# A two-block hybrid kernel on one core: the feed-forward computed token by token with its norm by halves, and the delta rule's output steps spread between attention work

## The chip, the cores and the metric

The kernel runs on one core of a Trainium2 chip. The metric is the time of one execution in microseconds on the device. Three executions of the kernel before gave 1759.13, 1759.20 and 1759.99 us, median 1759.2 us.

## The reference, cut to what matters

A first block of two layers (gated delta rule, latent attention and a gated linear recurrence side by side, then an output projection), then a second block of two layers, each with two feed-forwards around a mixer. There are 256 tokens of 1024 features, all in float32.

```python
# first block, in each layer: the delta rule in chunks
v_new = u_n - w_n @ state                       # per head
o = (q_n * exp(g_n)) @ state + a_n @ v_new
state = state * exp(g_last) + (k_n * exp(g_last - g_n)).T @ v_new
o_a = rmsnorm(o, gdn_out_norm) * silu(gz)
...
o_b = causal_block_attention(qf, kf, vm) * silu(mz)
x = x + concatenate([o_a, o_b, o_c]) @ w_out

# second block, in each layer l
x = x + 0.5 * swiglu(rms_norm(x, ffn1_norm[l]), gate, up, down)    # f10, f11
mem_n = rms_norm(mem, mem_norm[l])
...
x = x + mixed @ w_out[l]
x = x + 0.5 * swiglu(rms_norm(x, ffn2_norm[l]), gate, up, down)    # f20, f21
```

A swiglu is `(silu(h @ gate) * (h @ up)) @ down` with a hidden width of 2816, which the kernel takes as 11 blocks (`PAIRS`) of 256 columns. The first block's result also goes through `final_norm` before the second block reads it.

## The kernel before

The whole program is one list of steps, written out by hand in `schedule()`. Every engine walks the same list in the same order and does its own part of each step, so the list is at the same time the instruction order of TensorE, VectorE, ScalarE and GpSimd. Semaphores tie the engines together; an engine that waits holds up everything behind it in its own order.

Every float32 product with a weight is done as three products of reduced-width parts. A block of weights (1 MB) lands in `ring`; ScalarE rounds it into `weights_high` (two instructions, one for each half of the block), VectorE subtracts that from the original into `weights_rest` (again two), and TensorE multiplies high by high, high by rest and rest by high. `weights_high` has three places (`HIGHS`), the ring four, and five from the second block on. How far ScalarE and VectorE are ahead with this splitting is said at each step by `split_until(n)`: "everything up to block n, if not yet done".

Activations lie transposed, as 8 slices of 128 features by 256 tokens (`xT_high`, `xT_rest`). A norm step takes the mean square of both halves of the tokens (128 each), scales both, transposes both on TensorE (16 transposes), and then ScalarE and VectorE write the slices 256 tokens wide.

The feed-forward of before works feature by feature: block `g` (gate) and block `u` (up) give 256 hidden features by 256 tokens, each from 48 products that move 256 tokens past a piece of weights; ScalarE does the silu of `g`, VectorE multiplies by `u`, rounds (`CAST`) and subtracts, and the block `d` (down) is added into four PSUM banks by 24 products of 512 columns. On TensorE the down products of block j-1 stand behind gate and up of block j:

```python
for j in range(begin, pairs + 1 if end == pairs else end):
    ... gate and up of block j
    if j: ... pe.wait_ge(*at((id, "h", i))); accumulate(... i = j - 1 ...)
```

ScalarE's and VectorE's part of block j begins, for every j, with `split_until(split_no[(st, "g", j)] + 3)`. For j = 0 this is gate 0, up 0 and gate 1; for later j it is gate j, up j and down j-1. In `f10` and `f11` the norm of the memory tokens stands between the blocks: `norm_front` (squares, scales) ahead of block 5, and `norm_part` behind blocks 5 to 8.

The delta rule's output (`gdn_o`, once for each half n of the tokens) was one step each: on TensorE u, S and o for n = 0, or u, w, wS and o for n = 1, then the sum of squares of o. Between these products stand copies of PSUM results by ScalarE and one subtraction by VectorE. Attention of the first block has the steps `att` (scores; on VectorE mask and maximum), `sm` (exponential, division) and `pv` (transposes, values), and `mz` is a projection of 48 products.

In the profile's rows all ordinary products have line 784, transposes of a norm line 842, those of `pv` line 1147, the splitting on VectorE line 1889, and everything of ScalarE line 1377.

Of the kernel before, what the change touches and what calls it, by code (L numbers as in the profile page):

```python
# [16 lines left out]
F32 = mybir.dt.float32  # L17
F32R = mybir.dt.float32r
U32 = mybir.dt.uint32
ALU = mybir.AluOpType  # L20
# [3 lines left out]
P = 128  # L24
# [120 lines left out]
PAIRS = DFF // 256  # L145

# [6 lines left out]
def schedule():  # L153

    out = []
    for l in range(2):
        out.append(("norm", f"n{l}", "x", f"norm_gain{l}"))
        out.append(("ab", l))
        def proj(name, j=0):
# [10 lines left out]
                  32: (rots[0:3], rots[3:5]), 64: ([proj("mz", 0)], [])}  # L170
        out += [("tri", l, 0, 1), ("trid", l, 0, 1), proj("gz", 1), ("tri", l, 1, 1), ("trid", l, 1, 1)]
        for s in LEVELS[1:]:
            for n in range(2):
                out += [("tri", l, n, s)] + beside[s][n] + [("trid", l, n, s)]
        m = f"m{l}"
# [65 lines left out]
def weight_blocks(w):  # L241
# [12 lines left out]
    for st in schedule():  # L254
# [21 lines left out]
        elif kind == "ffn" and st[2] == 0:  # L276
# [71 lines left out]
def two_blocks(nc, w, out, old):  # L348
# [5 lines left out]
    half_at = block_no[(("ffn", "f10"), "g", 0)]  # L354
# [40 lines left out]
    with ctx:  # L395
# [251 lines left out]
        SLICES = (2, 3, 0, 1, 4, 5, 6, 7)  # L647

# [54 lines left out]
        def _(sp_eng):  # L703
# [6 lines left out]
            mem_at = block_no[(("ffn", "f10"), "g", 4)]  # L710
            for i, (key, pieces, _) in enumerate(blocks):
# [13 lines left out]
                if key == (("ffn", "f11"), "g", 4):  # L725
# [17 lines left out]
        def _(eng):  # L743
# [56 lines left out]
            def first_block(id, key, gkey, wv):  # L800

                banks = [group((*gkey, f)) for f in range(2)]
                wh_, wl_ = wv
                for n, k in enumerate(SLICES):
                    pe.wait_ge(*at(("xh", id, k)))
                    if k >= 4:
                        second_half(key)
                    for f in range(2):
                        for i, a in enumerate((wh_, wl_)):
                            mm(banks[f][:, 0:S], a[:, k, f * P:f * P + P], xh[:, k, :], n == 0 and i == 0, False)  # L810
                for n, k in enumerate(SLICES):
                    need_slice(n)
                    for f in range(2):
                        ins = mm(banks[f][:, 0:S], wh_[:, k, f * P:f * P + P], xl[:, k, :], False, n == KD - 1)
                ins.then_inc(*pe.mark(gkey, used=key))

# [13 lines left out]

            def st_norm(st):
# [3 lines left out]

                gs = [k // 2 for k in slices_of(st)[::2]]
                b = {g: group(("nt", id, g), among=range(4, 8) if id in ("f10", "f20", "f21") else None) for g in sorted(gs)}
# [156 lines left out]
            def st_gdn_o(st):  # L994
# [6 lines left out]
                ins.then_inc(*pe.mark(("u", l, n)))  # L1001
                if n == 0:
# [6 lines left out]
                else:  # L1009
                    pe.wait_ge(*at(("TTg", l)))  # L1010
                    b = group(("w", l))
                    for h in range(4):
                        ins = mm(b[:, h * P:h * P + P], ktm[:, 1, h, :], ET[:, 1, h, :])
                    ins.then_inc(*pe.mark(("w", l)))
                    pe.wait_ge(*at(("wT", l)))
                    pe.wait_ge(*at(("St", l)))
                    b = group(("wS", l))
# [1542 lines left out]
```

## Time and profile before

| | |
|---|---|
| median of three executions | 1759.2 us |
| the profiled execution, its own time | 1756.48 us |
| its span, first to last instruction | 1754.7 us |
| mean granted clock of TensorE | 0.974 |
| TensorE busy | 1661.3 us (95%) |
| VectorE busy | 1048.1 us (60%) |
| ScalarE busy | 872.9 us (50%) |

The span is nearly the time itself, and TensorE is busy in 95% of it. So the profile is read for the places at which TensorE has no work, for how fast its products follow each other where it has, and for its clock. In a timeline row the first number is the start and the second the duration in us; a duration includes the tail of the last product, so the rate of a stream is read from starts. The bracket gives the idle time just before, and what ended it.

### The profile page before, as it was taken

The page shows a single profiled execution, that of the slowest core. Times are in us where ns is not written, and L with a number is a line of the kernel's source. Part 1 is how long each engine was busy: PE and PEld are TensorE (multiplying, and loading weights), DVE is VectorE, ACT ScalarE, POOL GpSimd, SP SyncE. Part 2 cuts the span into 40 slices and gives each one's busy share as a digit, 9 for nine tenths or more (in the row PEclk, how much of TensorE's full clock was granted, in tenths as well). Part 3 has the DMA queues.
Part 4 walks back from the last instruction along what each step waited for, and adds up shares of the span by engine and source line. Part 5 has one row for each costly group of instructions (what it writes and reads, how often), then busy time and mean ns, then how long its engine had stood idle before and what let it go on. Part 6 is the DMA issues. An engine that isn't in the chain of part 4 may idle for free.

```text
span 1754.7 us, 27203 instructions
## 1 busy us (share of the span) xinstructions
PE 1661.3 (95%) x11578; PEld 1531.1 (87%) x11578; DVE 1048.1 (60%) x1506; ACT 872.9 (50%) x1297; POOL 97.7 (6%) x72
## 2 busy tenths in 40 slices
PE   7999899999989899999888999999999998789999
PEld 7989777989977799999887899989999997679998
DVE  6875564896646555555786645455646465555554
ACT  4975363686445435435445533344454357443332
POOL 0112000012200000000240000000000000000000
PEclk9999999999999899999999999998999999899999
DMA  7624224552313465555321555544665553035552
GB/s 224 191 66 135 71 73 145 157 158 89 97 49 117 163 213 191 171 190 169 121 83 62 168 186 179 188 140 135 196 204 175 185 169 120 24 113 179 190 192 97
DMA packets 204297, 253.24 MB, mean 144 GB/s; under 512 B 17808, under 2 KB 183952, under 8 KB 204048
## 3 DMA queue, kind: packets, MB, share of 16 engines
q1 hardware_dynamic: 204176, 251.49, 44.9%
q8 instruction: 92, 1.51, 0.4%
q14 instruction: 29, 0.24, 0.0%
HBM read 250.43 MB, written 1.05 MB: 143 GB/s over the span
## 4 chain that ended last, share of the span: by engine, by line
PE 78%; DVE 8%; ACT 6%; issue 5%; DMA 1%; POOL 1%; SPq 0%; DVEq 0%; ACTq 0%; POOLq 0%
PE bank L784 77%; ACT arena L1377 4%; DVE weights_rest L1889 2%; ACT weights_high L1377 1%; PE bank L842 1%; DVE arena L2036 1%; DMA ring<-in_w_in 1%; ACT L1377 1%; ACT L1372 1%; DVE small L2206 0%; DVE x L2252 0%; DVE weights_rest_more L1889 0%; DVE arena L2224 0%; POOL arena L2520 0%; DMA vec<-in_vec 0%
## 5 line engine op out<-in xcount | busy, mean ns | idle before, releaser
L784 PE MATMUL bank<-xT_high,weights_high 128*128 128x256 f32 (+1 forms) x2352 | 676.1, 288 | 8.9 <-DVE weights_rest L1889 4.1
L784 PE MATMUL bank<-xT_rest,weights_high 128*128 128x256 f32 (+1 forms) x2352 | 658.3, 284 | 0.0
L784 PE MATMUL bank<-xT_high,weights_rest 128*128 128x256 f32 (+1 forms) x2048 | 581.4, 285 | 0.0
L1889 DVE TENSOR_TENSOR weights_rest<-ring,weights_high 128x1024 fp32r<-128x1024 f32 (+3 forms) x414 | 486.6, 1225 | 98.8 <-ACT weights_high L1377 95.1
L1377 ACT ACTIVATE weights_high<-ring 128x1024 fp32r<-128x1024 f32 (+3 forms) x414 | 400.6, 1019 | 253.9 <-PE bank L784 235.6
L784 PEld LDWEIGHTS bank<-xT_high,weights_high 128*128 128x128 f32 (+1 forms) x2352 | 454.2, 193 | 19.4 <-issue 8.9
L784 PEld LDWEIGHTS bank<-xT_rest,weights_high 128*128 128x128 f32 (+1 forms) x2352 | 448.1, 192 | 3.5 <-issue 2.0
L784 PEld LDWEIGHTS bank<-xT_high,weights_rest 128*128 128x128 f32 (+1 forms) x2048 | 395.7, 193 | 0.6
L1377 ACT ACTIVATE arena<-bank 128x512 f32<-128x512 f32 (+4 forms) x253 | 134.5, 547 | 390.3 <-PE bank L784 327.4
L784 PE MATMUL bank<-arena 128*128 128x128 f32 (+2 forms) x1416 | 209.4, 307 | 37.3 <-ACT arena L1377 22.9
L784 PEld LDWEIGHTS bank<-arena 128*128 128x128 f32 (+1 forms) x1416 | 180.2, 203 | 63.6 <-ACT arena L1377 22.6
L2289 DVE TENSOR_TENSOR arena<-bank,arena 128x512 f32<-128x512 f32 x44 | 30.4, 692 | 321.3 <-PE bank L784 321.3
L784 PE MATMUL bank<-weights_high,arena_parts 128*128 128x512 f32 (+1 forms) x416 | 112.3, 379 | 0.9 <-DVE arena L2235 0.9
L784 PE MATMUL bank<-weights_high,hidden_high 128*128 128x512 f32 x352 | 96.3, 391 | 0.0
L784 PE MATMUL bank<-weights_high,hidden_rest 128*128 128x512 f32 x352 | 95.5, 389 | 0.0
L1377 ACT ACTIVATE weights_high<-ring_more 128x1024 fp32r<-128x1024 f32 x68 | 68.3, 1056 | 53.2 <-PE bank L784 53.1
L784 PEld LDWEIGHTS bank<-weights_high,arena_parts 128*128 128x128 f32 x416 | 76.4, 191 | 15.2 <-DVE arena L2235 1.0
L1889 DVE TENSOR_TENSOR weights_rest_more<-ring_more,weights_high 128x1024 fp32r<-128x1024 f32 x68 | 82.5, 1253 | 8.8 <-ACT weights_high L1377 7.9
L784 PE MATMUL bank<-xT_high,weights_rest_more 128*128 128x256 f32 x304 | 86.0, 283 | 0.0
L784 PEld LDWEIGHTS bank<-weights_high,hidden_rest 128*128 128x128 f32 x352 | 66.1, 188 | 14.2
L784 PE MATMUL bank<-weights_rest,hidden_high 128*128 128x512 f32 x272 | 73.4, 389 | 0.0
L784 PEld LDWEIGHTS bank<-weights_high,hidden_high 128*128 128x128 f32 x352 | 63.5, 189 | 11.1
(180 smaller groups left out, 1698.1 us busy)
## 6 DMA issues: line engine op xcount, KB each, us to landing
ring<-in_w_in SPq DMA_DIRECT2D x36, 1024.0 KB, 5.2
ring<-in_ffn_w_gate SPq DMA_DIRECT2D x36, 1024.0 KB, 5.4
ring<-in_ffn_w_up SPq DMA_DIRECT2D x35, 1024.0 KB, 5.4
ring<-in_ffn_w_down SPq DMA_DIRECT2D x34, 1024.0 KB, 4.9
ring<-in_w_out SPq DMA_DIRECT2D x22, 1024.0 KB, 4.9
ring<-in_w_in_a SPq DMA_DIRECT2D x11, 1024.0 KB, 5.2
ring_more<-in_ffn_w_down SPq DMA_DIRECT2D x10, 1024.0 KB, 5.1
ring_more<-in_ffn_w_up SPq DMA_DIRECT2D x9, 1024.0 KB, 5.3
```

Of the source, the lines that this page charges most:

```text
L784: return eng.matmul(o, a, b, start=first, stop=last)
L842: ins = eng.transpose(b[g][:, kk * S + t * P:kk * S + t * P + P], xs_of(st)[:, t, (2 * g + kk) * P:(2 * g + kk + 1) * P], ident)
L1372: eng.preload_act_table_set(need)
L1377: return eng.activation(dst, src, func, **kw_)
L1889: TTs(rest_slot(b)[:, part], raw_slot(b)[:, part], high_slot(key)[:, part].bitcast(F32), ALU.subtract).then_inc(*dv.mark(("rest", key, z)))
L2036: STT(out=cq[:, i, :], in0=cin[:, i, j:j + S], scalar=taps[:, j:j + 1], in1=cq[:, i, :], op0=ALU.mult, op1=ALU.add).then_inc(*dv.mark(*((( ...
L2289: TTs(h, ps(g, 2, S), h, ALU.mult).then_inc(*dv.mark((id, "h32", j), frees=g))
```

## The change

1. `schedule()`: `gdn_o` is cut into `gdn_u` (u, and w for n = 1), `gdn_w` (wS), `gdn_o` (S and o) and `gdn_n` (the norm of o), and `att` into `sc` (scores on TensorE) and `att` (the rest) for the first two head pairs. These steps are put between others.
2. Feed-forward: gate and up of a block come as two weight blocks (`g, j, 0` and `g, j, 1`), each with 4 of the 8 slices, 256 gate and 256 up columns side by side. The product is turned around: 128 tokens are the stationary side, and 512 weight columns move past them. The hidden values come out token by token and are transposed (4 transposes a block). ScalarE rounds them from PSUM, VectorE subtracts.
3. The norms ahead of `f10`, `f20` and `f21` are done by halves of the tokens: add, scale, transpose and slices of the first half, then its products of block 0, then the same for the second half. The norm ahead of `f11` stays as it was.
4. For block 0, ScalarE and VectorE now split 2 weight blocks ahead instead of 3.

```diff
-        out += [("gdn_o", l, 0), ("att", m, 0), ("sm", m, 0), proj("mz", 1), ("gdn_o", l, 1)]
+        out += [("gdn_u", l, 0), ("att", m, 0), ("sm", m, 0), proj("mz", 1), ("gdn_o", l, 0), ("gdn_u", l, 1)]
+        out += [("sc", m, 1), ("gdn_n", l, 0), ("gdn_w", l)]
...
+            if hp == 1:
+                out[-3:] = [("gdn_o", l, 1), ("sm", m, 1), proj("mz", 2), ("gdn_n", l, 1), ("parts", f"h{l}", *ready[1])]
...
-                cols((st, "g", j), w[f"{n}_w_gate_2"][l], 256 * j, 256 * j + 256)
-                cols((st, "u", j), w[f"{n}_w_up_2"][l], 256 * j, 256 * j + 256)
+                for z in range(2):
+                    pieces = [(w[f"{n}_w_{name}_2"][l].rearrange("(k p) n -> p k n", p=P)[:, 4 * z:4 * z + 4, 256 * j:256 * j + 256], c, c + 256)
+                              for name, c in (("gate", 0), ("up", 256))]
+                    out.append(((st, "g", j, z), pieces, (4, 512)))
...
+            def gate_up(st, j, z, t, b, order):
...
+                for n, k in order:
+                    if j == 0 and id in BY_TOKENS.values():
+                        pe.wait_ge(*at(("xl", id, t, k)))
+                    else:
+                        need_slice(n)
+                    if k % 4 >= 2:
+                        second_half(key)
+                    for i, (a, v) in enumerate(products(wv, [xh, xl])):
+                        ins = mm(b[:, 0:512], v[:, k, t * P:t * P + P], a[:, k % 4, :], n == 0 and i == 0, n == KD - 1 and i == 2)
...
+                for j in range(begin, end):
+                    b = [group((id, "gu", j, t)) for t in range(NT)]
+                    if j == 0 and id in BY_TOKENS.values():
...
+                        transposes(id, 1)
...
+                    else:
+                        for z in range(2):
+                            for t in range(NT):
+                                gate_up(st, j, z, t, b[t], order[4 * z:4 * z + 4])
+                            if j and z == 0:
+                                hidden_transposes(st, j - 1)
+                    if j == 1:
+                        open_acc(st)
+                    if j and j < pairs - 1:
+                        down(st, j - 1, (0, 1), (0, 1), used=True)
...
                 for j in range(begin, end):
-                    g = (id, "g", j)
-                    split_until(split_no[(st, "g", j)] + 3)
...
+                    split_until(split_no[(st, "g", j, 0)] + (3 if j else 2))
+                    if j:
+                        hidden_high(st, j - 1)
+                    for t in range(NT):
+                        g = (id, "gu", j, t)
+                        copy(sg[:, j % 2, t, :], g, ps(g, 2, S)[:, 0, :], (id, "s", j, t), func=ACT.Silu)
...
+            def add_and_norm(st, id):
...
+                add(0)
+                scale(0)
+                if id == "f20":
+                    split_until(n, more=1)
+                    slices(0, SLICES)
+                    add(1)
+                else:
+                    slices(0, SLICES[:4])
+                    add(1)
+                    split_until(n, more=1)
+                    slices(0, SLICES[4:])
+                split_until(n, more=2)
+                scale(1)
+                slices(1, SLICES)
```

**Order 1.** ScalarE (ACT) in `f21`, from the end of its norm to the silu of block 1. `weights_high` is the splitting; `arena2<-bank` is a silu (in before of gate alone, in after of each half of the tokens). Before:

```order
L1377 ACTIVATE weights_high<-ring 128x1024 [waits landed0,pe_outp]
L1377 ACTIVATE weights_high<-ring 128x1024
L1377 ACT_TABLE_LOAD
L1377 ACTIVATE arena2<-bank1 128x256 [waits pe_ffn]
L1377 ACTIVATE arena2<-bank2 128x256
L1377 ACTIVATE weights_high<-ring 128x1024 [waits landed1]
L1377 ACTIVATE weights_high<-ring 128x1024
L1377 ACTIVATE weights_high<-ring 128x1024 [waits landed2,pe_ffn]
L1377 ACTIVATE weights_high<-ring 128x1024
L1377 ACTIVATE arena2<-bank0 128x512 [waits pe_ffn]
```

The changed kernel, at the same place:

```order
L1430 ACT_TABLE_LOAD
L1430 ACTIVATE arena2<-bank1 128x256
L1430 ACTIVATE arena2<-bank2 128x256 [waits pe_ffn]
L1430 ACTIVATE weights_high<-ring 128x1024 [waits landed0,pe_outp]
L1430 ACTIVATE weights_high<-ring 128x1024
L1430 ACTIVATE weights_high<-ring 128x1024 [waits landed1]
L1430 ACTIVATE weights_high<-ring 128x1024
L1430 ACTIVATE weights_high<-ring 128x1024 [waits landed2]
L1430 ACTIVATE weights_high<-ring 128x1024
L1430 ACTIVATE hidden_high<-bank1 128x512 [waits pe_ffn]
```

The split of the weights that block 1 begins with (gate 1 before, `g, 1, 0` now) stood ahead of the first silu and stands behind both now. VectorE's order has moved in the same way.

**Order 2.** ScalarE in `f10` of the changed kernel, around `norm_front`, ahead of block 5. The first two rows are the silus of block 4, the last the rounded hidden values of block 4.

```order
L1430 ACTIVATE arena2<-bank0 128x256 [waits pe_ffn]
L1430 ACTIVATE arena2<-bank1 128x256 [waits pe_ffn]
L1425 ACT_TABLE_LOAD
L1430 ACTIVATE arena2,small<-arena2 128x1024 [waits mem_in]
L1430 ACTIVATE small<-small 128x1 [waits act_norm_front] x2
L1430 ACTIVATE arena2,small<-arena2 128x1024 [waits act_norm_front]
L1430 ACTIVATE small<-small 128x1 [waits act_norm_front] x2
L1430 ACTIVATE weights_high<-ring_more 128x1024 [waits landed4,act_norm_front]
L1430 ACTIVATE weights_high<-ring_more 128x1024
```

Before, the same work stood behind a silu that waited for gate alone; now it stands behind one that waits for gate and up of the whole block.

**Order 3.** TensorE (PE) at the delta rule's output, layer 0, 128x128 float32 products (`bank<-arena`), from u and w of the second half on. Before:

```order
L784 MATMUL bank6<-arena 128x128 [waits dve_trid]
L784 MATMUL bank6<-arena 128x128 x3
L784 MATMUL bank7<-arena 128x128 [waits dve_trid]
L784 MATMUL bank7<-arena 128x128 x3
L784 MATMUL bank0<-arena 128x128 [waits act_gdn_o]
L784 MATMUL bank0<-arena 128x128 x3
L784 MATMUL bank1<-arena 128x128 [waits dve_gdn_a,dve_gdn_o]
L784 MATMUL bank1<-arena 128x128 x7
L784 MATMUL bank2<-arena,const 128x512 [waits act_gdn_o]
```

The changed kernel, from S and o of the first half (banks 3 and 4) to the second transposes of `pv`:

```order
L791 MATMUL bank4<-arena 128x128 x4
L791 MATMUL bank5<-arena 128x128 [waits dve_trid]
L791 MATMUL bank5<-arena 128x128 x3
L791 MATMUL bank6<-arena 128x128 [waits dve_att,dve_trid]
L791 MATMUL bank6<-arena 128x128 x3
L791 MATMUL bank7<-arena 128x128 [waits dve_att]
...
L791 MATMUL bank1<-arena,const 128x512 [waits act_gdn_o]
L791 MATMUL bank2<-arena 128x128 [waits act_proj,act_gdn_o]
L791 MATMUL bank2<-arena 128x128 x3
L1166 MATMUL bank3<-const,arena 128x128 [waits dve_sm]
L1166 MATMUL bank3<-const,arena 128x128
L1166 MATMUL bank4<-const,arena 128x128 [waits dve_gdn_o,dve_sm]
```

The scores (banks 7 and 0) now stand between w and wS (bank 2), the values of pair 0 between wS and o; and the last row takes bank 4, in which o of the first half lies until VectorE has read it.

## Rows read from the trace of the kernel before

**Rows 1.** The page: its head and the engines' busy time

```profile
span 1754.7 us, 27203 instructions
...
PE 1661.3 (95%) x11578; PEld 1531.1 (87%) x11578; DVE 1048.1 (60%) x1506; ACT 872.9 (50%) x1297; POOL 97.7 (6%) x72
```

**Rows 2.** Windows, in f21: PE, PEld, DVE, ACT, POOL busy, clock, DMA share, GB/s

```profile
1650.00:1675.00 25.00, 25.00 (x176) 23.51 (x176) 11.59 (x14) 10.39 (x11) 0.00 (x0) 1.00 0.57 186
```

**Rows 3.** TensorE's timeline in f21: down, gate and up, the next down

```profile
1654.88 1.09 PE L784 MATMUL bank<-weights_high,hidden_high 128*128 128x512 f32 x4
...
1660.34 0.28 PE L784 MATMUL bank<-xT_high,weights_high 128*128 128x256 f32 x1
...
1671.86 1.09 PE L784 MATMUL bank<-weights_high,hidden_high 128*128 128x512 f32 x4
```

**Rows 4.** TensorE's timeline: products after an idle stretch

```profile
978.73 1.94 PE L842 MATMUL bank<-const,arena 128*128 128x128 f32 x16 [3.27 <-DVE arena L1956]
...
1170.95 2.70 PE L842 MATMUL bank<-const,arena 128*128 128x128 f32 x16 [3.27 <-DVE arena L1956]
...
1560.53 3.14 PE L842 MATMUL bank<-const,arena 128*128 128x128 f32 x16 [3.27 <-DVE arena L1956]
```

**Rows 5.** Timelines of ScalarE and VectorE: a split of one block; a silu

```profile
1549.30 1.99 ACT L1377 ACTIVATE weights_high<-ring 128x1024 fp32r<-128x1024 f32 x2
...
1550.37 2.36 DVE L1889 TENSOR_TENSOR weights_rest<-ring,weights_high 128x1024 fp32r<-128x1024 f32 x2 [0.52 <-ACT weights_high L1377]
...
1569.88 0.66 ACT L1377 ACTIVATE arena<-bank 128x256 f32<-128x256 f32 x2 [1.47 <-PE bank L784]
```

**Rows 6.** ScalarE's timeline in f10 around the front of the memory norm

```profile
674.64 0.60 ACT L1377 ACTIVATE arena<-bank 128x512 f32<-128x512 f32 x1 [3.80 <-PE bank L784]
675.26 1.28 ACT L1372 ACT_TABLE_LOAD   x1
...
680.05 2.01 ACT L1377 ACTIVATE weights_high<-ring_more 128x1024 fp32r<-128x1024 f32 x2
```

**Rows 7.** Timelines at the starts of f10, f20 and f21, TensorE and VectorE

```profile
591.19 1.29 DVE L2252 SCALAR_TENSOR_TENSOR x<-bank,x 128x512 f32<-128x512 f32 x2 [4.79 <-PE bank L784]
...
598.18 1.63 PE L842 MATMUL bank<-const,arena 128*128 128x128 f32 x8 [4.28 <-DVE arena L2309]
...
604.00 0.55 PE L784 MATMUL bank<-xT_high,weights_high 128*128 128x256 f32 x1 [1.16 <-DVE xT_high L1977]
...
629.21 1.09 PE L784 MATMUL bank<-weights_high,hidden_high 128*128 128x512 f32 x4
...
973.43 1.28 DVE L2252 SCALAR_TENSOR_TENSOR x<-bank,x 128x512 f32<-128x512 f32 x2
...
1003.79 1.09 PE L784 MATMUL bank<-weights_high,hidden_high 128*128 128x512 f32 x4
...
1554.57 1.29 DVE L2252 SCALAR_TENSOR_TENSOR x<-bank,x 128x512 f32<-128x512 f32 x2 [1.83 <-PE bank L784]
...
1586.96 1.09 PE L784 MATMUL bank<-weights_high,hidden_high 128*128 128x512 f32 x4
```

**Rows 8.** Timelines at the delta rule's output, layer 0, TensorE and VectorE

```profile
192.49 2.05 PE L784 MATMUL bank<-arena 128*128 128x128 f32 x16 [0.75 <-ACT arena L1377]
195.23 2.05 PE L784 MATMUL bank<-arena 128*128 128x128 f32 x16 [0.69 <-ACT arena L1377]
197.97 1.12 PE L784 MATMUL bank<-arena,const 128*128 128x512 f32 x2 [0.69 <-ACT arena L1377]
...
201.87 0.69 DVE L2162 TENSOR_TENSOR arena<-bank,arena 128x512 f32<-128x512 f32 x1 [6.17 <-ACT arena L1377]
...
213.22 2.07 PE L784 MATMUL bank<-arena 128*128 128x128 f32 x8 [2.42 <-ACT arena L1377]
216.14 3.71 PE L784 MATMUL bank<-arena 128*128 128x128 f32 x16 [0.85 <-DVE arena L2155]
220.53 1.13 PE L784 MATMUL bank<-arena,const 128*128 128x512 f32 x2 [0.69 <-ACT arena L1377]
```

More of the change, by code:

```diff
@@ L647, in two_blocks @@
         SLICES = (2, 3, 0, 1, 4, 5, 6, 7)
+        BY_TOKENS = {"h1": "f10", "s0": "f20", "s1": "f21"}
         def slices_of(st):
@@ L834, in st_norm @@
                     eng.wait_ge(sems("ident_in"), 16)
+                if id in BY_TOKENS.values():
+                    transposes(id, 0)
+                    return
                 gs = [k // 2 for k in slices_of(st)[::2]]
-                b = {g: group(("nt", id, g), among=range(4, 8) if id in ("f10", "f20", "f21") else None) for g in sorted(gs)}
+                b = {g: group(("nt", id, g)) for g in sorted(gs)}
                 for t in range(NT):
@@ L1415, in st_final @@
                 for t in range(NT):
[L1416 to L1417 removed]
+                    one = slice(t, t + 1)
+                    ac.wait_ge(*at(("x_ready", id, t)))
+                    A(final_sq if id == "f10" else xs2[:, t, :], x[:, t, :], ACT.Square, accum_out=ss[:, one]).then_inc(*ac.mark(("ss", id, t)))
                     ac.wait_ge(*ac.last())
[L1419 removed]
@@ L1877, in split_until @@
             def split_until(n, ahead=0, more=0):
-                n = 2 * min(reach((pieces[0] + 1) // 2, n, ahead), len(split)) + more
+                n = 2 * min(reach((pieces[0] + 1) // 2, n, ahead) if ahead else n, len(split)) + more
                 while pieces[0] < n:
@@ new lines, in add_acc, with slices, add @@
+            def add_acc(st, scale):
+                added = [add_half(st, t, scale) for t in range(NT)]
+                for nx in sched[place[st] + 1:]:
+                    if nx[0] == "norm" and nx[2] == "x":
+                        for t in range(NT):
+                            new.at[("x_ready", nx[1], t)] = added[t]
+                        break
+            def add_and_norm(st, id):
+                gain = next(nx[3] for nx in sched if nx[0] == "norm" and nx[1] == id)
+                n = (pieces[0] + 1) // 2 + 1
+                split_until(n)
+                def slices(t, ks):
+                    for k in ks:
+                        v = ps(("nt", id, t, k // 2), 2, P)
+                        src, g = v[:, k % 2, :], V(gain)[:, k:k + 1]
+                        to = slice(t * P, t * P + P)
+                        if k == 2:
+                            dv.wait_ge(*at(("nt", id, t, 1)))
+                            for q in (2, 3):
+                                TS(xh[:, q, to], v[:, q % 2, :], V(gain)[:, q:q + 1], None, ALU.mult).then_inc(*dv.mark())
+                            dv.wait_ge(*dv.last())
+                        if k not in (2, 3):
+                            dv.wait_ge(*at(("xh", id, t, k)))
+                            dv.wait_ge(*at(("xh", id, t, k ^ 1)))
+                        STT(out=xl[:, k, to], in0=src, scalar=g, in1=xh[:, k, to].bitcast(F32), op0=ALU.mult,
+                            op1=ALU.subtract).then_inc(*dv.mark(("xl", id, t, k), frees=("nt", id, t, k // 2)))
+                def add(t):
+                    new.at[("x_ready", id, t)] = add_half(st, t, 1.0)
+                    if id == "f10":
```

337 lines of the change are left out of this document (181 added, 156 removed).

## The prediction

> **What bounds the kernel.** I read the page first: TensorE is busy for 95% of the span and no other engine for more than 60% [rows 1]. Then the windows: inside a feed-forward TensorE is busy for 25.00 of 25 us at full clock, while VectorE and ScalarE have less than half of the time filled and the transfers 0.57 of theirs [rows 2]. So a steady block costs what TensorE's instructions cost, and everything else is a matter of places where TensorE has nothing to do. Those I took from its timeline: before the norms of f10, f20 and f21 [rows 7], and in the delta rule's output [rows 8]. After an idle stretch comes a second price: the same 16 transposes behind the same 3.27 us of idling took 1.94, 2.70 and 3.14 us [rows 4], since the clock had sometimes fallen to its lower level.
>
> **Steady blocks.** From 1654.88 to 1660.34 TensorE does the 24 products of down, 0.2275 us each; from there to 1671.86 the 96 products of gate and up with 256 columns, 0.120 us each, 11.52 us together [rows 3]. The new gate and up are 48 products of 512 columns, of the shape of down: 48 x 0.2275 = 10.92 us. That saves 0.60 us a block. It adds 4 transposes of 128x128: 16 took 1.94 us warm, of which about 0.28 is the tail of the last [rows 3, 4], so 0.11 each and 0.44 a block. 44 blocks in four feed-forwards; three block 0s are counted with the starts below: 41 x 0.60 = 24.6 saved, 44 x 0.44 = 19.4 paid, **-5.2 us**. The Trainium skill has this otherwise (TensorE: Matmul & The Clock Gate, section Back-to-back issue gap): 262 cycles for 256 columns and 518 for 512, or 0.109 and 0.216 us at 2.4 GHz. By that gate and up would go from 10.5 to 10.4 us, 0.1 saved instead of 0.6, and 41 blocks would be some 20 us dearer than in my sum. The row has 0.120 for 256 columns, so I keep the row.
>
> In the steady state nothing else reaches TensorE, as I lay it out. The weights of the next block are split behind the silu that ends a block, 0.33 + 3.43 us (below), under 5.46 us of down. Hidden values have 5.4 us of second-half gate and up over them. At the end of a feed-forward the rounding and subtraction, some 1.3 us, lie beside 6 products of down (1.37 us); uncovered they would cost 5 us in all. The transfers are 88 more issues of half the size, with the landing one ring place ahead and the queue idle most of the time: no cost, and 0.4 us each if they ever stood in line.
>
> **Block 1 of each feed-forward.** Here I see a new wait. Order 1: the split of the weights of block 1 stands behind both silus of block 0, on ScalarE and on VectorE, and TensorE's first product takes slice 2, for which it asks for both halves of the split. Down begins only behind block 1, so between block 0 and block 1 TensorE has nothing at all. The chain: silu of the second half 0.33 us (half of 0.66), then ScalarE's start to VectorE's end of one block 1549.30 to 1552.73, 3.43 us [rows 5]; with signals 3.8 us. Before, gate 1 was split ahead. Four times 15.2 us. After 3.8 us of idling the clock probably falls. What that costs: in the transposes alone 0, 0.76 and 1.20 us in the three cases of [rows 4], and in the delta rule 2.7 us (below). I take 1.7, with 0 and 2.7 as ends: 6.8 us. Together **+22.0 us**. The queue behind this wait on TensorE is all of the feed-forward; nothing hides it.
>
> **Block 5 of f10 and f11.** Order 2: the front of the memory norm stands on ScalarE between the silu of block 4 and the split for block 5. From the end of the silu at 675.24 to the start of the split at 680.05 it takes 4.81 us [rows 6]. It used to follow the silu of gate, with up (5.76 us) and down (5.46) still before TensorE; now it follows the end of the whole block. 0.33 + 4.81 + 3.43 = 8.6 us against 5.46 us of down: 3.1 us of wait, and 1.7 for the clock: twice, **+9.6 us** (6.2 without the clock, 11.6 with 2.7).
>
> **The starts by halves.** f10 idles 4.28 + 1.06 + 1.16 us before its first product, f20 and f21 3.27 us before their transposes [rows 4, 7]. Block 0 was finished 11.52 us before the first down: 617.69, 992.27 and 1575.44 [rows 7]. In the new order the first half goes from its add (591.19, 973.43, 1554.57) through square, scale, 8 transposes and slices, and TensorE starts its 24 products about 6 to 7 us after the add in f10, where the gain of the final norm is multiplied in, and 5 to 6 in the others; but VectorE does add, split and slices of both halves one after the other, so the second half's transposes come only 15 us (f10) and 12 us behind the add, and 24 x 0.2275 = 5.5 us of products behind those. That ends block 0 at about 613.4, 992.3 and 1573.5: **-6.2 us** in all (f10 -4.3, f20 0, f21 -1.9). The ends: 0, and all of the idling above, 13 us. For f20 the add starts late, behind a split, and in the new order it is followed by one more split piece and all eight slices before the second half's add; so I expect nothing there. f11 keeps its norm but loses the pass over the high parts that began before the rests were ready: **+0.5**.
>
> **The delta rule's output.** Before, TensorE waits 0.75 + 0.69 + 0.69 + 2.42 + 0.85 + 0.69 = 6.09 us in a layer, and runs slowly for a while: the 8 records of wS take 2.07 us where 16 took 2.05, the 16 of o 3.71 [rows 8], so 1.0 + 1.7 = 2.7 us more. 8.8 us a layer; the second layer shows the same rows. Order 3: the scores (16 records) and the projections now cover the first four waits and the last. But the second transposes of pv take bank 4, where o of the first half lies until VectorE has read it. From the end of the sum of squares at 199.09 to VectorE's start at 201.87 are 2.78 us, and 0.69 for the reading [rows 8]; wS and two transposes cover 1.3 of these 3.5 us. Then o of the second half waits for wS to be subtracted, on VectorE behind the whole norm of the first half. I put 3.0 us of waits and 1.2 of slow clock (between 0 and 2.7): 4.6 us gained a layer, **-9.2 us** (ends -5 and -17.6).
>
> **Sum.** -5.2 + 22.0 + 9.6 - 6.2 + 0.5 - 9.2 = +11.5 us. The profiled execution took 1756.48 us, 1.8 more than its span, so it would take 1768.0; the median of the runs is 2.7 us above it, and 1759.2 + 11.5 = 1770.7 us.
>
> **Rivals.**
> - Clock unhurt: the six new waits are there but the clock stays up. As after 978.73, where 16 transposes took 1.94 us [rows 4]; against it are the other two cases and longer waits now. 11.5 - 10.2 = +1.3: 1760.5 us.
> - Faster: block 1 isn't starved. If the split of its weights were finished while TensorE is still in the second half of block 0, 22.0 us fall away: 1748.7 us. It decides where wait and clock together cost less than 2.6 us in a feed-forward instead of 5.5. For it: only three short instructions are in the chain. Against: Order 1 puts them behind a silu that needs the last product of block 0.
> - Every block starved: 3.8 us of chain under 5.46 us of down leave 1.7 us. If the new order (silu in two parts, rounding on ScalarE) makes the chain 0.5 us too long, 36 blocks cost 18 us: 1789 us. Against it: ScalarE has 10.39 us of work in 25 [rows 2].
> - Turned products no cheaper: 256 columns pace at their 512-column rate, so gate and up saves 0.1 us a block; 20 us dearer, 1791 us. That is the rule above; the row speaks against it.
>
> **How the numbers follow.** About 0.2%, 3.5 us, can be told from no change. Forecast (waits of 3 to 4 us with clock, partial gains): 0.56, its own range 1763 to 1779. Clock unhurt 0.16, faster rival 0.12, every block starved 0.12, no cheaper products 0.04. The range leaves out the faster rival's centre and the last two: 1751 to 1787. Faster: the rival's 0.12, some of the case with the clock up and of larger gains in the starts and the delta rule, 0.20. Same 0.14, slower 0.66.
>
> **What would show it.** A block period (down to down) of 16.8 us instead of 16.98. An idle stretch of about 3.8 us before the first product of block 1 in each of four feed-forwards, released by VectorE's split, and of about 3.1 us ahead of block 5 in f10 and f11. In the delta rule one wait of about 2.2 us inside pv's transposes, released by VectorE, and no 2.42 us wait. First downs of f10 and f21 would be 2 to 5 us earlier relative to the output projection, were there no wait before block 1. I am wrong if TensorE runs through from block 0 to block 1, or if the block period isn't below 16.98.

## The result and the profile after

Five executions of the changed kernel took 1764.13 to 1767.94 us, median 1765.56; five of the kernel before, in the same comparison, 1751.16 to 1759.99, median 1759.13. The ratio is 1.0048, with a 95% interval of 1.0025 to 1.0071: slower, by 6.4 us of median against the 11.5 that I had forecast. The execution that was profiled took 1767.94 us, 11.5 more than the profiled one of before. Two later comparisons of the same two kernels gave 1.0104 and 1.0095 (below), so the cost is somewhere from 6 to 17 us, and the first comparison shows the low end of it. The forecast lies between them.

The page of the changed kernel, its head and busy times, to be read beside [rows 1]:

```profile
span 1766.0 us, 23513 instructions
...
PE 1659.5 (94%) x9642; PEld 1437.4 (81%) x9642; DVE 1044.2 (59%) x1536; ACT 904.0 (51%) x1399; POOL 97.7 (6%) x72
```

TensorE has 1936 instructions fewer: 48 products in place of 96 in each of 44 blocks, less four transposes added to each. Its busy time falls by only 1.8 us, since the products that are left have twice the columns, and 0.2275 us each instead of 0.120 [rows 3]. The mean granted clock hardly moved, 0.972 against 0.974. A stretch inside f21, of the same length as [rows 2], as windows (columns as there):

```profile
1625.00:1650.00 25.00, 25.00 (x116) 20.69 (x115) 9.65 (x11) 8.51 (x13) 0.00 (x0) 1.00 0.55 184
```

The steady state is as before: TensorE is full, at full clock. The list of what TensorE waited for (engine and line, the total in us, how often, the longest) shows what is new:

```profile
PE bank L791 <- DVE weights_rest L1968: 14.0, 5, 3.9
PE bank L791 <- DVE weights_rest_more L1968: 11.5, 4, 3.9
...
PE bank L1166 <- DVE arena L2244: 5.0, 2, 2.5
```

Waits for split weights took 4.1 us in all before and take 25.5 now. TensorE's timeline in f10, between block 0 and block 1:

```profile
598.84 0.39 PE L791 MATMUL bank<-weights_rest,xT_high 128*128 128x512 f32 x1
603.13 0.63 PE L791 MATMUL bank<-weights_high,xT_high 128*128 128x512 f32 x1 [3.91 <-DVE weights_rest L1968]
603.56 0.63 PE L791 MATMUL bank<-weights_high,xT_rest 128*128 128x512 f32 x1
```

3.9 us without work, and then a product every 0.43 us instead of 0.2275. ScalarE and VectorE at the same place:

```profile
599.26 0.38 ACT L1430 ACTIVATE arena<-bank 128x256 f32<-128x256 f32 x1 [2.27 <-PE bank L791]
599.54 3.88 ACT L1430 ACTIVATE weights_high<-ring 128x1024 fp32r<-128x1024 f32 x4
...
600.63 4.63 DVE L1968 TENSOR_TENSOR weights_rest<-ring,weights_high 128x1024 fp32r<-128x1024 f32 x4 [0.52 <-ACT weights_high L1430]
```

The silu of block 0's second half starts when TensorE has stopped, and the split of block 1's weights comes behind it: the chain of the forecast, piece by piece. The windows of the wait, of what follows, and of the next 10 us:

```profile
599.23:603.13 3.90, 0.00 (x0) 0.03 (x1) 2.93 (x4) 3.87 (x5) 0.00 (x0) 1.00 1.08 361
603.13:606.55 3.42, 3.42 (x9) 2.68 (x9) 3.42 (x4) 2.19 (x3) 0.00 (x0) 0.52 0.31 102
606.55:616.20 9.65, 9.65 (x45) 7.98 (x44) 2.09 (x3) 0.98 (x2) 0.00 (x0) 0.99 0.34 110
```

The third number from the right is the granted clock: 0.52 of full speed for 3.4 us behind the wait, then full again. The same timeline ahead of block 5, ScalarE first, then TensorE:

```profile
666.80 0.38 ACT L1430 ACTIVATE arena<-bank 128x256 f32<-128x256 f32 x1 [2.34 <-PE bank L791]
667.21 1.28 ACT L1425 ACT_TABLE_LOAD   x1
...
671.99 2.00 ACT L1430 ACTIVATE weights_high<-ring_more 128x1024 fp32r<-128x1024 f32 x2
...
671.14 1.07 PE L791 MATMUL bank<-weights_rest,hidden_high 128*128 128x512 f32 x4
675.59 0.77 PE L791 MATMUL bank<-weights_high,xT_high 128*128 128x512 f32 x1 [3.38 <-DVE weights_rest_more L1968]
```

Where the 11.3 us between the two spans lie, stage by stage, from starts in the two timelines, with an output projection taken at the end of its last product. "First" and "last down" are the first products of down behind block 1 and block 10:

| stage | before | after | difference |
|---|---|---|---|
| start to last output projection of the first block | 593.90 | 579.81 | -14.1 |
| from there to f10's first down | 35.31 | 36.40 | +1.1 |
| f10, first to last down | 154.55 | 159.71 | +5.2 |
| mixer, layer 0 | 191.25 | 193.65 | +2.4 |
| from there to f20's first down | 28.78 | 34.67 | +5.9 |
| f20, first to last down | 152.82 | 151.22 | -1.6 |
| f20's last down to f11's first | 92.29 | 98.46 | +6.2 |
| f11, first to last down | 154.56 | 158.39 | +3.8 |
| mixer, layer 1 | 153.35 | 152.58 | -0.8 |
| from there to f21's first down | 30.15 | 34.15 | +4.0 |
| f21, first to last down | 152.82 | 151.22 | -1.6 |
| f21's last down to the end | 14.92 | 15.74 | +0.8 |

### The profile page after: what moved, and what is told of

Read it like the earlier page. It is cut to its first block, busy times and chain, and to the rows that moved or that the text cites. A ratio compares the mean times of both kernels' runs of the same rounds, so it can differ in the third digit from the quotient of the medians.

```text
span 1766.0 us, 23513 instructions
## 1 busy us (share of the span) xinstructions
PE 1659.5 (94%) x9642; PEld 1437.4 (81%) x9642; DVE 1044.2 (59%) x1536; ACT 904.0 (51%) x1399; POOL 97.7 (6%) x72
## 4 chain that ended last, share of the span: by engine, by line
PE 56%; DVE 6%; ACT 4%; issue 1%; POOL 1%; DVEq 0%; ACTq 0%; POOLq 0%
PE bank L791 54%; ACT arena L1430 2%; DVE weights_rest L1968 2%; PE bank L1220 1%; DVE weights_rest_more L1968 1%; ACT weights_high L1430 1%; PE bank L847 1%; ACT L1425 0%; DVE small L2288 0%; DVE x L2333 0%; POOL arena L2649 0%; DVE xT_rest L2365 0%; DVE arena L2306 0%; DVE arena L2528 0%; POOL arena L2648 0%
## 5 line engine op out<-in xcount | busy, mean ns | idle before, releaser
L791 PE MATMUL bank<-weights_high,xT_high 128*128 128x512 f32 (+2 forms) x880 | 340.7, 393 | 34.8 <-DVE weights_rest_more L1968 11.5
L791 PE MATMUL bank<-weights_high,xT_rest 128*128 128x512 f32 (+2 forms) x816 | 311.0, 381 | 0.0
L791 PE MATMUL bank<-xT_high,weights_high 128*128 128x256 f32 (+1 forms) x944 | 276.8, 293 | 6.0 <-DVE xT_rest L2062 3.1
L791 PE MATMUL bank<-xT_rest,weights_high 128*128 128x256 f32 (+1 forms) x944 | 269.6, 286 | 0.0
L791 PE MATMUL bank<-weights_rest,xT_high 128*128 128x512 f32 (+2 forms) x696 | 262.3, 383 | 0.0
L791 PE MATMUL bank<-xT_high,weights_rest 128*128 128x256 f32 (+1 forms) x912 | 260.4, 285 | 0.0
L791 PE MATMUL bank<-arena 128*128 128x128 f32 (+3 forms) x1416 | 204.2, 304 | 29.4 <-ACT arena L1430 17.1
L791 PEld LDWEIGHTS bank<-xT_high,weights_high 128*128 128x128 f32 (+1 forms) x944 | 182.4, 193 | 13.4 <-issue 6.2
L791 PEld LDWEIGHTS bank<-xT_rest,weights_high 128*128 128x128 f32 (+1 forms) x944 | 182.3, 193 | 2.4 <-issue 2.0
L791 PEld LDWEIGHTS bank<-xT_high,weights_rest 128*128 128x128 f32 (+1 forms) x912 | 175.8, 193 | 0.6
L791 PEld LDWEIGHTS bank<-weights_rest,xT_high 128*128 128x128 f32 x696 | 133.7, 192 | 25.6
L1430 ACT ACTIVATE hidden_high<-bank 128x512 fp32r<-128x512 f32 x44 | 26.3, 599 | 166.8 <-PE bank L1220 166.8
```

The source lines that it names most:

```text
L791: return eng.matmul(o, a, b, start=first, stop=last)
L1430: return eng.activation(dst, src, func, **kw_)
```

## The experiments

The ratios are to the kernel before, measured beside it on the same chip. There were three chips. The two repairs, both together and the filler ran on the first. The changed kernel again, the two runs on the delta rule's part and the one on the bank of o ran on the second. The changed kernel a third time, both repairs again and the last two experiments ran on the third.

### One more block split ahead in block 0

```diff
-                    split_until(split_no[(st, "g", j, 0)] + (3 if j else 2))
+                    split_until(split_no[(st, "g", j, 0)] + 3)
```

> The kernel after, with one number changed: in block 0 of each feed-forward ScalarE and VectorE split three weight blocks ahead instead of two, so that the first weight block of block 1 is ready before block 0 ends. My theory (block 1 is starved by this split, and the clock falls behind the wait): the idle 3.90 us and the slow 1.6 us behind it go in all four feed-forwards, so 22 us less than after, about 1744 us and a ratio to before near 0.991. Rival 1 (the third split goes on ScalarE between the norm's slices and the silu and delays the start of block 0 or the silu by as much as it saves): within 5 us of after, 1761 to 1766. Rival 2 (the wait goes, the clock does not come back): 15.6 us less, about 1750.

Median 1745.2 us, ratio 0.9967 (0.9954 to 0.9981). Against the changed kernel's 1.0104 and 1.0095 that is 1.3% or 23 us less: my theory. (The expected ratio of 0.991 was missed only because the kernel before took 1752.0 us here, not 1759.) TensorE's timeline at block 1 of f10 has:

```profile
599.58 0.39 PE L791 MATMUL bank<-weights_rest,xT_high 128*128 128x512 f32 x1
601.02 0.47 PE L791 MATMUL bank<-weights_high,xT_high 128*128 128x512 f32 x1 [1.06 <-DVE weights_rest L1968]
```

1.06 us are left in f10, where ScalarE also does the final norm, and none in the other three; the products behind it come at full rate. In the trace the four stages that end at a first down are 4.2, 3.8, 6.6 and 5.8 us shorter; of f11's 6.6, 0.8 lie ahead of its norm, so the start itself gained 5.8 as well. f20 gets only 3.8, since in this execution the clock fell earlier, in block 0. Two windows of f20:

```profile
967.53:971.94 4.41, 4.41 (x10) 3.45 (x11) 3.99 (x10) 1.63 (x5) 0.00 (x0) 0.50 0.07 26
971.94:993.60 21.66, 21.23 (x99) 17.41 (x98) 12.48 (x21) 10.57 (x18) 0.00 (x0) 1.00 0.44 146
```

### One block split ahead of the memory norm's front

```diff
+                if st[2] == "mem":
+                    split_until(splits[0] + 1)
```

(on ScalarE; VectorE has the same with its own counter)

> The kernel after, with one weight block more split ahead of the front of the memory norm in f10 and f11 on ScalarE and VectorE (behind the silu of block 4, before the squares). My theory (block 5 is starved because its split stands behind 4.8 us of norm): the two idles of 3.38 us and the slow stretches behind them (2.9 and 1.7 us) go, 11 us less than after, about 1754 us. Rival (the norm's front is then late and delays a later block or the memory transposes by the same): no more than 3 us less than after.

Median 1758.72, ratio 1.0043 (1.0032 to 1.0055), 0.57% or 10 us less than the changed kernel in the two later comparisons. Both waits are gone, and first to last down takes 153.18 and 153.16 us in f10 and f11 instead of 159.71 and 158.39: 11.8 us. At block 5 TensorE's timeline now runs through:

```profile
669.72 1.07 PE L791 MATMUL bank<-weights_rest,hidden_high 128*128 128x512 f32 x4
670.62 0.39 PE L791 MATMUL bank<-weights_high,xT_high 128*128 128x512 f32 x1
```

### Both

> The kernel after with both edits: three weight blocks ahead in block 0 of each feed-forward, and one ahead of the front of the memory norm. My theory adds the two: 33 us less than after, about 1733 us, a ratio to before near 0.985. Rival (the two share something, such as weight blocks that land too late when both are split early): less than 28 us.

Median 1737.03, ratio 0.9917 (0.9905 to 0.9929). Once more, with the changed kernel on the same chip:

> Both repairs once more (three weight blocks ahead in block 0, one ahead of the memory norm's front), beside the next kernel on one chip. Ratio 0.992, as the first time; between 0.989 and 0.994 if only the clock's differences from one execution to the next are added.

Median 1737.93, ratio 0.9910 (0.9896 to 0.9923), against 1770.99 of the changed kernel: 33.1 us less. The two repairs add, 23 and 10 us; the difference is the expected 33, and the expected 1733 us was counted from the first comparison's lower median of the changed kernel, 1765.56.

### The wait filled with products

```diff
+                    if j == 1:
+                        for _ in range(16):
+                            mm(b[0][:, 0:512], xh[:, 0, 0:P], xh[:, 0:2, :].rearrange("p a b -> p (a b)"))
```

> The kernel after with work added and no wait taken away: ahead of block 1 of each feed-forward TensorE does 16 more products of 512 columns (about 3.6 us) whose result is overwritten by the block's own first product, so they lie inside the wait of 3.90 us. If the slow 1.6 us behind the wait come from the idling, the clock stays up and the kernel gains up to 6 us over after, about 1760 us. If the clock does not hang on the idling, or the slow records are something else, the time is that of after within 1 us.

TensorE's timeline, and the windows of the filler and of what follows:

```profile
597.31 3.79 PE L791 MATMUL bank<-xT_high 128*128 128x512 f32 x16
601.38 0.47 PE L791 MATMUL bank<-weights_high,xT_high 128*128 128x512 f32 x1 [0.28 <-DVE weights_rest L1971]
601.69 0.40 PE L791 MATMUL bank<-weights_high,xT_rest 128*128 128x512 f32 x1
```

```profile
597.31:601.10 3.79, 3.79 (x17) 2.82 (x15) 2.65 (x3) 3.59 (x5) 0.00 (x0) 1.00 1.07 356
601.38:605.00 3.62, 3.62 (x16) 3.02 (x17) 3.62 (x4) 2.20 (x3) 0.00 (x0) 1.00 0.31 102
```

The weights come as late as before, but the clock stays at 1.00 in all four places, and the three starts that begin behind an output projection are 1.6 us shorter each. Median 1765.02, ratio 1.0072 (1.0059 to 1.0085), 0.28% or 5 us under the changed kernel in its two later comparisons. So the slow stretch belongs to the idling: filling the wait with useless work wins back the price of the slow stretch, though not the wait.

### The changed kernel again

> The kernel after once more, unchanged, so that the kernels of this call stand against it on one chip. Its ratio to before was 1.0048 (1.0025 to 1.0071); the sum of the two profiled executions gives 1.0064. The mechanical account (waits and clock read from the traces) gives +11 us, a ratio of 1.0063; if the earlier interval's centre is right, 1.0048.

> The kernel after a third time, unchanged. Its two comparisons so far gave 1.0048 and 1.0104, with intervals that do not meet, while its own median moved little (1765.6 and 1769.4) and that of before moved more (1759.1, 1752.0, 1752.9). Theory: the mean granted clock differs from one execution to the next (0.970 to 0.980 for the same kernel before), 0.001 of it is about 1.7 us, and the result of one comparison carries some 5 us of that. Then this gives a ratio between 1.005 and 1.011. If a property of the first session alone was the cause, 1.010 again.

Medians 1769.37 and 1770.99, ratios 1.0104 (1.0083 to 1.0125) and 1.0095 (1.0079 to 1.0110). The interval of the first comparison doesn't meet either. The kernel before had medians of 1752.0, 1752.85 and 1754.2 us on the three chips of the experiments (38 executions) and 1759.13 in the first comparison, where four of its five lay at 1757.85 to 1759.99 and one at 1751.16. Among the 38 the time goes with the mean granted clock: 1760.74 us at 0.971 and 1760.23 at 0.970, 1749.13 to 1753.84 in the executions at 0.979; a straight line through all 38 gives 1.0 us for 0.001 of clock, not the 1.7 expected above. The profiled execution of before had 0.974, and the clocks of the others in the first comparison aren't on record. So it is likely, not shown, that part of the difference between the comparisons is how often the clock fell in the kernel before; the changed kernel's own median also rose, by 3.8 and 5.4 us. The third ratio, 1.0095, fits both of the expectations above and doesn't decide between them. What set the first comparison apart stays open.

### The delta rule's part alone, and all but it

In the kernel before:

```diff
-        out += [("gdn_o", l, 0), ("att", m, 0), ("sm", m, 0), proj("mz", 1), ("gdn_o", l, 1)]
+        out += [("gdn_u", l, 0), ("att", m, 0), ("sm", m, 0), proj("mz", 1), ("gdn_o", l, 0), ("gdn_u", l, 1)]
+        out += [("sc", m, 1), ("gdn_n", l, 0), ("gdn_w", l)]
```

with all the steps and functions that this needs, and in the changed kernel:

```diff
-        out += [("gdn_u", l, 0), ("att", m, 0), ("sm", m, 0), proj("mz", 1), ("gdn_o", l, 0), ("gdn_u", l, 1)]
-        out += [("sc", m, 1), ("gdn_n", l, 0), ("gdn_w", l)]
+        out += [("gdn_u", l, 0), ("gdn_o", l, 0), ("gdn_n", l, 0), ("sc", m, 0), ("att", m, 0), ("sm", m, 0), proj("mz", 1)]
+        out += [("gdn_u", l, 1), ("gdn_w", l), ("gdn_o", l, 1), ("gdn_n", l, 1), ("sc", m, 1)]
```

> The kernel before with the first part of the change alone: the delta rule's output and the scores cut into steps and spread; feed-forward and norms as before. If the gain of the delta rule that the traces show (7.4 and 6.7 us in the two layers) is its own, this is 14 us faster than before, a ratio of 0.992. If my prediction's size (4.6 a layer) is right, 9 us, 0.995. If part of the gain came from the feed-forward's change or from the chip's drift, less than 9.

> The kernel after without the first part of the change: the steps of the delta rule's output stand as in the kernel before, feed-forward and norms as after. If the parts add, this is 14 us slower than after, 25 us slower than before, a ratio of 1.014; by my prediction's sizes 20.7 us slower than before, 1.012.

The spread alone: median 1743.45, ratio 0.9945 (0.9928 to 0.9963), 9.4 us of median less than before. Without it: 1779.17, ratio 1.0153 (1.0127 to 1.0178), 9.8 us more than the changed kernel on the same chip. That is my forecast's 9.2, not the 14 that the traces suggested. The traces of the two kernels without the spread come from executions 3.6 and 4.3 us above their medians (1756.48 against 1752.85, 1783.45 against 1779.17), which would be most of the gap. For the second the place shows: in its trace the clock is low from 213.0 to 230.1 us, and the stretch between the first layer's early and late output projections takes 83.6 us, against 79.3 in before and 73.8 in the changed kernel. For the first it stays an argument. The rest of the change, then, costs 25.9 us (1743.45 to 1769.37), or 26.3 (1752.85 to 1779.17), where I had 20.7. TensorE's timeline of the changed kernel at the first pv, and VectorE's read that lets it go on:

```profile
210.93 0.38 PE L1166 MATMUL bank<-const,arena 128*128 128x128 f32 x2
213.81 0.77 PE L1166 MATMUL bank<-const,arena 128*128 128x128 f32 x4 [2.50 <-DVE arena L2244]
...
231.67 1.57 PE L791 MATMUL bank<-arena 128*128 128x128 f32 x12 [0.97 <-ACT arena L1430]
...
212.97 0.69 DVE L2244 TENSOR_TENSOR arena<-bank,arena 128x512 f32<-128x512 f32 x1 [8.38 <-ACT arena L1430]
```

The third row is a wait that before didn't have, 0.97 us ahead of the values of the second pv, released by ScalarE. o of the second half doesn't wait: it follows the values of the first pv without a gap. Together this is 3.5 us of wait a layer where there were 6.09 [rows 8].

### The transposes off the bank of o

```diff
-                    b = group(("pt", name, hp, t))
+                    b = group(("pt", name, hp, t), among=[i for i in range(8) if i != new.bank[("o", int(name[1]), 0)]] if (name[0], hp) == ("m", 0) else None)
```

> Both repairs of the feed-forward (three weight blocks ahead in block 0, one ahead of the memory norm's front) and, in the delta rule, the transposes of the first pv kept out of the PSUM bank that holds o of the first half. The wait of 2.50 us before pv's second transposes is released by VectorE's reading of that bank: if the bank is its cause it goes in both layers, 5 us less than with the repairs alone, a ratio of about 0.989 instead of 0.992. Rival: another bank or VectorE's next read holds it as long, and nothing changes, 0.992.

Median 1734.68, ratio 0.9906 (0.9886 to 0.9926), the same as without it. TensorE's timeline:

```profile
210.78 0.82 PE L1166 MATMUL bank<-const,arena 128*128 128x128 f32 x6
213.57 1.60 PE L791 MATMUL bank<-arena 128*128 128x128 f32 x12 [1.97 <-DVE arena L2248]
216.09 1.16 PE L791 MATMUL bank<-arena 128*128 128x128 f32 x8 [0.91 <-DVE arena L2238]
```

All six transposes run on, and the values behind them wait for the same read of VectorE (1.97 us), then o for VectorE's subtraction (0.91). One bank later the same thing is late; the wait is moved, not removed. What this trace does differently is the clock: it stays at 1.00 behind both waits in both layers, and the layers are 1.1 and 1.0 us shorter for it. The timed runs don't tell whether that is the edit's doing or this execution's.

### A projection ahead of pv

```diff
             if hp == 1:
-                out[-3:] = [("gdn_o", l, 1), ("sm", m, 1), proj("mz", 2), ("gdn_n", l, 1), ("parts", f"h{l}", *ready[1])]
+                out[-4:] = [proj("mz", 2), ("pv", m, 0), ("gdn_o", l, 1), ("sm", m, 1)]
+            if hp == 2:
+                out[-4:-4] = [("gdn_n", l, 1), ("parts", f"h{l}", *ready[1])]
```

> Both repairs, and in the first block two steps moved: the third mz projection (48 products, some 11 us) goes ahead of the first pv, and the norm of o of the second half goes behind the scores of the third head pair. If the waits of 2.50 and 0.97 us in each layer come from VectorE standing behind the norm of o's first half, they are covered: 7 us less than with the repairs alone, 0.988. If the steps moved leave another wait of the same length (the pv products behind ScalarE's exponential, or the sum of squares behind its square), 0.992 again.

A miss: median 1745.03, ratio 0.9945 (0.9931 to 0.9960), 7.1 us more than the repairs alone on the same chip. TensorE, then ScalarE:

```profile
229.03 0.82 PE L1168 MATMUL bank<-const,arena 128*128 128x128 f32 x6
234.51 1.86 PE L793 MATMUL bank<-arena 128*128 128x128 f32 x7 [4.66 <-ACT arena L1432]
...
233.13 1.06 ACT L1432 ACTIVATE arena_parts<-arena 128x1024 fp32r<-128x1024 f32 x1 [1.46 <-DVE arena L2253]
234.09 0.85 ACT L1432 ACTIVATE arena<-bank 128x256 f32<-128x256 f32 x2
```

The wait at the first pv went (0.31 us is left), but the rounding of the delta rule's output (`parts`), which must follow its norm, now stands ahead of ScalarE's copies for the second pv, and itself waits for VectorE: 4.66 us where 0.97 had been. So a layer waits 4.97 us instead of 3.47, 3.0 us more in the two. In the trace the two layers' stretches are 1.5 and 2.5 us longer than with the repairs alone; the 1.0 beyond the waits is the clock's, which was low for 6.8 us in the second layer's stretch instead of 3.4. The trace's other 3.8 us lie in its first 130 us, where no step was moved and where traces of the same code differ as much (128.3 to 132.5 us). What makes up the last 3 of the 7 us in the timed runs stays open.

### Halves for f10 alone

```diff
-        BY_TOKENS = {"h1": "f10", "s0": "f20", "s1": "f21"}
+        BY_TOKENS = {"h1": "f10"}
...
-                    split_until(splits[0] + (1 if id == "s0" else 2))
+                    split_until(splits[0] + 2)
```

> The kernel after with the norm by halves kept for f10 alone; the norms ahead of f20 and f21 are done as in the kernel before, 16 transposes and slices 256 tokens wide (and ScalarE splits two weight blocks behind the last output projection of s0, as in before). The terms of my sum for these two starts are 0 and -1.9 us, so this is 1.9 us slower than after, and the stretch from the output projection to the first down of f20 stays within 0.5 us. If the halves are worth the idle of 3.27 us that they replace, 4 to 5 us slower. If by halves is dearer there (more transposes in pieces, more waits), 1 to 3 us faster.

Median 1773.53, ratio 1.0114 (1.0100 to 1.0128) beside the changed kernel's 1.0095 (1.0079 to 1.0110): the intervals touch. The traces say it more finely: to f20's first down 34.82 us instead of 34.67, to f21's 35.89 instead of 34.15, where block 0 ends 18.7 us behind the projection instead of 17.0. The halves are worth nothing in f20 and 1.7 us in f21.

## Why the prediction was right

- **Block 1 of each feed-forward (+22.0).** Right in mechanism and size. The wait was 3.90 us in all four (I had 3.8), released by VectorE's split, and the slow stretches behind cost 1.6 us each (I had 1.7): 22.0 us. Counted from starts it is 5.8 us a place, 23.2 in all, because the tail of the last product ahead of the wait and the first products behind it cost another 0.3, which I had left out. Shown by the first experiment, and the clock's share of it by the filler. The rivals "clock unhurt" and "block 1 isn't starved" fall.
- **Block 5 of f10 and f11 (+9.6).** Right in mechanism, a little small: waits of 3.38 us (I had 3.1), slow stretches that cost 2.9 and 1.7 (I had 1.7 each), 11.3 us by the rows, 11.8 by the second experiment's trace.
- **Steady blocks (-5.2).** Right. The period is 16.80 us against 16.98, and first to last down is 1.6 us shorter where no wait lies between. TensorE's timeline in f21, two downs apart by one block, beside [rows 3]:

```profile
1649.44 0.39 PE L791 MATMUL bank<-weights_high,hidden_high 128*128 128x512 f32 x1
...
1666.26 0.39 PE L791 MATMUL bank<-weights_high,hidden_high 128*128 128x512 f32 x1
```

  The rival that every block starves falls with them. So does the one on the price of columns: by the rule of the Trainium skill (TensorE: Matmul & The Clock Gate, section Back-to-back issue gap) gate and up would have gained only 0.1 us a block and the four transposes have cost 0.44, so that the period would have grown; it shrank. What I costed at nothing there isn't quite nothing: at the end of each feed-forward the last rounding and subtraction lie beside 6 products and leave 0.4 us open, 1.6 in all:

```profile
1753.34 0.71 PE L791 MATMUL bank<-weights_high,hidden_high 128*128 128x512 f32 x2
1753.89 0.63 PE L791 MATMUL bank<-weights_high,hidden_rest 128*128 128x512 f32 x2
1754.36 0.62 PE L791 MATMUL bank<-weights_rest_more,hidden_high 128*128 128x512 f32 x2
1755.10 0.70 PE L791 MATMUL bank<-weights_high,hidden_high 128*128 128x512 f32 x2
```

- **The starts by halves (-6.2).** From the last output projection to the end of block 0, f10 gained 4.5 us, f20 lost 0.25, f21 gained 1.6 (I had 4.3, 0 and 1.9). f11 lost 0.6 (I had 0.5): its block 0 ends 19.4 us behind its transposes as before, though the products are 0.6 us shorter. The loss is a new wait of 0.68 us, six products into block 0, for the rests that VectorE writes.
- **The delta rule's output (-9.2).** Right in size when the kernels are timed (-9.4 alone, 9.8 when it is taken out), with the main wait in the place that I had named, inside the first pv's transposes, released by VectorE: 2.50 us where I had 2.2. The rest of the 3.0 us of waits that I had forecast was at the wrong place. o of the second half doesn't wait, and the values of the second pv do, for ScalarE (0.97 us); that the two nearly cancel is luck. My end of -5 us doesn't follow from its terms either: 8.8 less 3.0 and 2.7 is 3.1 a layer, -6.2. The pair of traces had put the gain at 14.1, half as much again as the term; the timed runs withdraw that.
- **The sum (+11.5).** It equals the difference of the two profiled executions, but by luck. In that pair of traces the first block gained 14.1 us, not 9.2, and the rest cost 25.4, not 20.7, and the two misses cancel. Against the later comparisons (16.5 and 16.8 us of median) the sum is some 5 us too small. The delta rule's term holds there, so the gap is in the feed-forward's part, 26 us where I had 20.7. The traces show where it lies: block 5 cost 2.2 more than I had, block 1 1.2 more, the open ends 1.6, and the starts and steady blocks differ by a few tenths. In place, the four starts, the blocks and the ends take 25.6 us more than before (26.3 and 26.4 in the changed kernel's two other traces).

  The repaired kernel shows the same from the other side: with the repairs it lies 0.28 to 0.35%, 5 to 6 us, under the kernel with the spread alone, where steady blocks, starts and f11 promised 10.9. Its two traces give 6.3 and 6.8 us in place. Of what is missing, 1.6 are the open ends, 1.4 the wait that is left in f10, and 1.5 to 2.0 the low clock in f20's block 0.
- **The base.** The forecast of 1770.7 us started from a median of 1759.2, which no later comparison of the kernel before reached; the changed kernel's own medians were 1765.56, 1769.37 and 1770.99. That the last two lie so near 1770.7 is luck too: a base 5 to 7 us high and a sum some 5 us small.

## What to carry to other kernels

When a producer's look-ahead is counted in pieces, count again when the size of a piece or its consumer's order changes: here one number (2 instead of 3 blocks), needed at four places, cost 23 us, and with it and one line ahead of a side task mended, the same change turns from 17 us slower to 16 us faster than the kernel before. Price a wait of some 4 us on TensorE together with the slow products behind it, 1.3 to 2.9 us here, and 0.3 us for the tail and the restart. And check a sum term by term: a total that agrees can be two misses. And when a wait moves instead of going, look at which read is late, not at which bank or step is waiting for it.

## What I had not expected of the hardware

- In six profiled executions of kernels with the 3.90 us wait (the changed kernel three times, and those with the memory norm mended, without the spread, and with halves for f10 alone) a slow stretch followed all 24 of these waits, 2.7 to 6.1 us long. It doesn't always begin at once: behind the wait that ends at 991.14 the first five products of the changed kernel still come at the full rate, and the slow ones begin at 992.37. All 14 waits of 3.38 us ahead of block 5, in the seven traces that have them, were followed by one too. Behind idle stretches of 3.27 us the same had come and gone from one place to the next [rows 4].
- The 38 later executions of the kernel before have mean granted clocks of 0.970 to 0.980 and took 1749.13 to 1760.74 us, a spread wider than what this change costs in the first comparison. A profiled execution is one draw from that; two traces can show a difference of 14 us for a part that timed runs put at 9.5.
- The clock's fall can move when a wait is removed: with the first repair f20 runs its block 0 slowly (2.1 us lost) where it had run block 1 slowly (1.6). It needn't: in the trace of the run with the transposes off the bank of o, whose feed-forward is the repaired one, the clock doesn't fall there, and f20's first down comes 28.91 us behind the projection instead of 30.92.
